# Identities of the two inverse buffers written by GpSimd, the first level ahead of the mirrored buffer, and VectorE copies over two PSUM banks

## The chip, the cores and the metric

The kernel runs on one core of a Trainium2 chip. The metric is the device time of one execution in microseconds. TensorE (PE) multiplies matrices into PSUM, VectorE (DVE) and ScalarE (ACT) read PSUM and SBUF, GpSimd (POOL) works on SBUF, and SyncE (SP) issues the loads and stores. Each engine works through its own instructions in the order written, and waits on semaphores for the others.

## The reference

Two blocks follow each other. The first has two hybrid attention layers; the change doesn't touch it. The second is a trunk layer with two recurrent branches over 512 tokens (256 of a context, 256 of a grid), each in two directions `d`, then a merge and an MLP.

```python
# branch A (rwkv7): 16 heads of 64
S_t = S_{t-1} diag(w_t) - (S_{t-1} kk_t) b_t^T + v_t k_t^T ;  y_t = S_t r_t
# branch B (gated delta rule), 8 heads of 128, in chunks of 64:
a_mat = tril(kb @ k^T * decay, -1) + I
sol = triangular_solve(a_mat, rhs)            # lower, unit diagonal
```

Both recurrences are evaluated chunk by chunk, and each chunk needs the inverse of a unit triangular matrix. These inverses are what the change is about.

## The kernel before

The program has stages L (first block), P (projections into `z_kept`), B (the recurrences) and C/M (merge and MLP). Stage B lasts from about 1890 to 2820 us of the span.

Stage B runs eight threads woven round robin by `Weave` on each engine: `thread_a(0)`, `thread_b(0)`, `thread_a(1)`, `thread_b(1)`, two tails and two bases. `thread_a(d)` goes over eight pairs of heads `c`, `thread_b(d)` over eight heads `h`; a thread of `d == 1` starts an inverse once the thread of `d == 0` is some steps into its own. Each engine's generator of a thread yields at the same places, so the weave alone fixes the order of the work on each engine, and the semaphores only hold it up. One round (two inverses of each branch) takes about 111.7 us and comes eight times.

An inverse of branch A (`inverse_a`, 8 blocks of 128, so 128x512 buffers) works on X (the inverse) and XP (its transpose, the *mirrored* buffer), both of which lie over buffers that the scores read before (Kd, Bd):

- VectorE copies an identity from `cst` into X and XP (L2734), after the last score matmuls (`sR`) and transposes (`tBt`).
- It writes level 0 into XP from NA (SBUF) by four predicated copies (L2742), then level 0 into X from PSUM by one (L2747), once TensorE has done the products `iq` of level 0, which move NA's diagonal blocks.
- For the levels 1 to 5, TensorE forms `iq` = NA X, VectorE takes the masked part into Q (L2759, one predicated copy for each of the thread's two banks), TensorE forms `it` (both products XP Q and Q XP), and ScalarE and VectorE share the copies back into X and XP (L1836, L1837, L2764, L2765). GpSimd restores Q to an identity (L3358) and at the end copies a part of XP into XT (L3362).

The inverse of branch B (`inverse`, 128x256) has the same steps: identities L2687, mirrored level 0 in L2694, level 0 of X in L2703. There X and XP lie over `g.gl`, which VectorE reads for NA (L2953); GpSimd writes `g.gl` and masks `g.dec` beforehand (L3404, L3407). The scores of branch A are masked out of PSUM in `scores` (L2855: two copies of 128x512 for NA and two for AK; L2863: four of 128x256 for RB and RK). The base tile's mixing of the next pair's tokens stands in L2601 and L2608.

In this document *iq0* and *iq1* are the `iq` products of levels 0 and 1, *Q1* is VectorE's masked copy of level 1, and *it1* the products that need it. The queue order on TensorE around the start of an A inverse is: score matmuls `sR`, iq0, matmuls of other threads, iq1, matmuls of other threads, it1.

```python
for x in (X, XP):                                            # L2733
    e.tensor_copy(x.rearrange("p (u s) -> p u s", u=8), bc(C("id64"), 8)).then_inc(*mark(V))
```

Of the kernel before, what the change touches and what calls it, by code (L numbers as in the profile page):

```python
# [6 lines left out]
F32 = mybir.dt.float32  # L7
# [241 lines left out]
def program(nc, W, WSM, LORA, PARd, CSTd, MSKd, CTX, XIN, XS, ZS, OUT):  # L249
    ctx = ExitStack()  # L250
    with ctx:  # L251
# [12 lines left out]
        banks = [ctx.enter_context(nc.psum_tensor(f"bank{i}", [128, 512], F32))[:, :] for i in range(8)]  # L264
# [289 lines left out]
        STRAIGHT = (slice(0, 4, 3), slice(0, 4, 2))  # L554
        CROSSED = (slice(1, 3), slice(1, 4, 2))

        def staying(lv):
            return slice(0, 2) if lv < 5 else slice(0, 4, 2)

        def moving(lv):  # L560
            return slice(2, 4) if lv < 5 else slice(1, 4, 2)

        def units(pairs):
            return [2 * s + i for s in range(4)[pairs] for i in range(2)]
# [3 lines left out]
        def tensor(e):  # L568
# [428 lines left out]
            def inverse(tag, ring, NA, X, XP, Q, n):  # L997
# [52 lines left out]
            def inverse_a(tag, ring, NA, X, XP, Q):  # L1050
# [23 lines left out]
                yield  # L1074
                for lv in range(1, 6):
                    straight, crossed = units(STRAIGHT[lv % 2]), units(CROSSED[lv % 2])
                    stay, move = units(staying(lv)), units(moving(lv))
                    w.wait_ge(done("X", tag, lv - 1))
                    w.wait_ge(done("Xc", tag, lv - 1)) if lv > 1 else None
                    b0, b1 = bank(), bank()  # L1080
                    for i in range(4):
                        u, v = straight[i], crossed[i]
                        for h in range(2):
                            mm(b0[halves[h], cols(i)], block(u, h), X[halves[h], cols(u)], True, True)
                        for h in range(2):
                            t = mm(b1[halves[1 - h], cols(i)], block(v, h), X[halves[h], cols(v)], True, True)
# [5 lines left out]
                    b0, b1 = bank(), bank()  # L1092
                    q = Q[lv % 2]
                    for i in range(4):
                        u, v = straight[i], crossed[i]
                        for h in halves:
                            mm(b0[h, cols(i)], XP[h, cols(u)], q[h, cols(u)], True, True)
                        for h in range(2):
                            mm(b1[halves[1 - h], cols(i)], XP[halves[h], cols(v)], q[halves[h], cols(v)], True, True)
                    for i in range(4):  # L1100
                        u, v = stay[i], move[i]
                        for h in halves:
                            mm(b0[h, cols(4 + i)], q[h, cols(u)], XP[h, cols(u)], True, True)
                        for h in range(2):
                            t = mm(b1[halves[1 - h], cols(4 + i)], q[halves[h], cols(v)], XP[halves[h], cols(v)], True, True)
# [305 lines left out]
        def scalar(e):  # L1411
# [412 lines left out]
            def inverse_a(tag, ring, X, XP, XT):  # L1824
# [5 lines left out]
                for lv in range(1, 6):  # L1830
                    ring.take(), ring.take()
                    yield
                    (b, u), _ = ring.take(), ring.take()
                    wd = 1 << lv
                    w.wait_ge(done("it", tag, lv))
                    cp(pairs(X, 4, wd, d)[:, STRAIGHT[lv % 2]], pairs(b[:, 0:256], 2, wd, d)).then_inc(*mark(V, "X", tag, lv))  # L1836
                    cp(pairs(XP, 4, wd, 1 - d)[:, staying(lv)], pairs(b[:, 256:512], 2, wd, 1 - d)).then_inc(*mark(V, "free", ring.name, u))  # L1837
                    counts.at[("XT", tag, lv)] = counts.last(V)
# [307 lines left out]
        def vector(e):  # L2146
# [531 lines left out]
            def inverse(tag, ring, NA, X, XP, XT, Q, n, sem, before):  # L2678
# [5 lines left out]
                for point in before:  # L2684
                    w.wait_ge(point)
                for x in (X, XP):
                    e.tensor_copy(x.rearrange("p (u s) -> p u s", u=n), bc(C("id64"), n)).then_inc(*mark(sem))  # L2687
                own(sem)
                m0 = M("xt0", d * 32, 32)[:, None, :].broadcast_to([128, n, 32])
                for h in (0, 64):  # L2690
                    hs = slice(h, h + 64)
                    xv = XP[hs, :].rearrange("p (u n two) -> p u n two", u=n, two=2)[:, :, :, 1 - d]
                    nv = NA[hs, :].rearrange("p (u n two) -> p u n two", u=n, two=2)[:, :, h // 2:h // 2 + 32, 1 - d]
                    e.copy_predicated(xv, m0[hs], nv).then_inc(*mark(sem))  # L2694
                counts.at[("XT", tag, 0)] = counts.last(sem)
                for lv in range(6):
# [5 lines left out]
                    if lv == 0:  # L2702
                        e.copy_predicated(region(X, wd, d), mk, src).then_inc(*mark(sem, "free", ring.name, u))  # L2703
                        counts.at[("X", tag, 0)] = counts.last(sem)
                        yield
# [21 lines left out]
            def inverse_a(tag, ring, NA, X, XP, XT, Q, before):  # L2727
# [3 lines left out]
                for point in before:  # L2731
                    w.wait_ge(point)
                for x in (X, XP):  # L2733
                    e.tensor_copy(x.rearrange("p (u s) -> p u s", u=8), bc(C("id64"), 8)).then_inc(*mark(V))  # L2734
                own(V)
                for h in range(2):
                    hs = slice(64 * h, 64 * h + 64)
                    nv = NA[hs, :].rearrange("p (s u n two) -> p s u n two", s=4, u=2, two=2)[:, :, :, 32 * h:32 * h + 32, 1 - d]
                    m0 = M("xt0", d * 32, 32)[hs, None, None, :].broadcast_to([64, 2, 2, 32])
# [1105 lines left out]
```

## Time and profile before

| | |
|---|---|
| median of 3 runs | 3774.3 us (3773.59 to 3777.36) |
| the profiled execution | 3773.41 us, of which its span 3771.5 us |
| mean granted TensorE clock | 0.975 |
| PE, PEld busy | 95%, 83% of the span |
| DVE, ACT, POOL busy | 59%, 40%, 44% |

A row of the timeline is: start, duration, engine, line, operation, out<-in, how many in the row, and in brackets how long the engine sat idle before it and on whom it waited. A row of several instructions has the time from the first one's start to the last one's end; neighbouring instructions of one engine can overlap, since the next begins before the last has drained. All numbers are microseconds unless said otherwise.

### The profile page before, as it was taken

What the parts mean: (1) busy time and instruction counts of PE and PEld (TensorE: products, weight loads), DVE (VectorE), ACT (ScalarE), POOL (GpSimd) and SP (SyncE); (2) the same over time, 40 slices, a digit from 0 to 9 for tenths busy, and PEclk for the clock granted to TensorE, in tenths of its full rate; (3) what the DMA queues carried; (4) which work ended last, traced back from release to release, by engine and by line L of the source; (5) the groups of instructions that cost most, each with busy time, mean ns of one, the idle gap of its engine ahead of it and who ended that gap; (6) DMA issues with size and microseconds to landing.
All of it is one profiled execution on the core that took longest, in us unless ns stands there. A gap on an engine that the chain in (4) does not pass through costs nothing. (4 is left out here: it accounts for less than half of the span.)

```text
span 3771.5 us, 79181 instructions
## 1 busy us (share of the span) xinstructions
PE 3575.4 (95%) x33504; PEld 3118.9 (83%) x33504; DVE 2224.6 (59%) x4232; ACT 1521.8 (40%) x2753; POOL 1651.4 (44%) x1195
## 2 busy tenths in 40 slices
PE   7999998999997999999979999999979999999998
PEld 6888787888786888888868878888869898989897
DVE  4645535655536776677666677666656654445443
ACT  4444434444435432232223333333334453535353
POOL 5555455555554543333321111111116566666664
PEclk9999999999999999999989999999999999999999
DMA  6445554444344777778610000000006445455543
GB/s 229 183 168 189 186 196 156 178 179 181 146 176 168 257 268 257 252 257 292 215 40 18 24 28 29 25 24 15 3 33 254 174 179 190 179 190 180 188 180 134
DMA packets 116368, 586.83 MB, mean 156 GB/s; under 512 B 20912, under 2 KB 40368, under 8 KB 51376
## 3 DMA queue, kind: packets, MB, share of 16 engines
q1 hardware_dynamic: 116016, 581.76, 42.2%
q8 instruction: 267, 4.37, 0.5%
q14 instruction: 85, 0.70, 0.1%
HBM read 561.00 MB, written 20.71 MB: 154 GB/s over the span
## 5 line engine op out<-in xcount | busy, mean ns | idle before, releaser
L574 PE MATMUL bank<-act_L,part_L 128*128 128x512 f32 (+1 forms) x4864 | 935.4, 347 | 9.2 <-DMA cst<-in_cst 4.8
L574 PEld LDWEIGHTS bank<-act_L,part_L 128*128 128x128 f32 x4864 | 756.1, 191 | 146.4 <-issue 28.1
L574 PE MATMUL bank<-act_P,part_P 128*128 128x512 f32 (+1 forms) x3488 | 716.4, 365 | 17.5 <-POOL part_P L3221 12.6
L3221 POOL TENSOR_TENSOR part_C<-wring,part_C 128x512 fp32r<-128x512 f32 x320 | 567.8, 1783 | 362.3 <-ACT part_C L1420 362.3
L3221 POOL TENSOR_TENSOR part_L<-wring,part_L 128x512 fp32r<-128x512 f32 x304 | 526.2, 1732 | 446.1 <-ACT part_L L1420 438.2
L574 PEld LDWEIGHTS bank<-act_P,part_P 128*128 128x128 f32 x3488 | 590.3, 188 | 136.9 <-DVE arena_P L2590 16.1
L574 PE MATMUL bank<-arena_B 64*64 64x64 f32 (+2 forms) x11200 | 446.0, 237 | 51.1 <-DVE arena_B L2747 24.8
L3221 POOL TENSOR_TENSOR part_P<-wring,part_P 128x512 fp32r<-128x512 f32 x184 | 306.3, 1670 | 427.7 <-ACT part_P L1420 427.7
L1420 ACT ACTIVATE part_C<-wring 128x1024 fp32r<-128x1024 f32 x320 | 338.0, 1057 | 347.9 <-PE bank L574 345.7
L574 PE MATMUL bank<-act_Y,part_C 128*128 128x258 f32 (+1 forms) x3840 | 464.8, 283 | 9.4 <-POOL part_C L3221 9.4
L574 PEld LDWEIGHTS bank<-act_Y,part_C 128*128 128x128 f32 x3840 | 463.9, 191 | 9.8 <-issue 9.6
L574 PEld LDWEIGHTS bank<-arena_B 64*64 64x64 f32 (+2 forms) x11200 | 380.7, 147 | 103.5 <-DVE arena_B L2747 27.2
L574 PE MATMUL bank<-act_C,part_C 128*128 128x512 f32 (+1 forms) x2560 | 459.6, 340 | 0.0
L574 PEld LDWEIGHTS bank<-act_C,part_C 128*128 128x128 f32 x2560 | 391.6, 188 | 58.0
L1420 ACT ACTIVATE part_L<-wring 128x1024 fp32r<-128x1024 f32 x304 | 320.7, 1056 | 255.6 <-PE bank L574 255.0
L2167 DVE TENSOR_TENSOR part_L<-wring,part_L 128x512 fp32r<-128x512 f32 x304 | 248.2, 816 | 254.7 <-ACT part_L L1420 253.5
L2167 DVE TENSOR_TENSOR part_C<-wring,part_C 128x512 fp32r<-128x512 f32 x320 | 235.0, 734 | 252.2 <-ACT part_C L1420 245.4
L2167 DVE TENSOR_TENSOR part_P<-wring,part_P 128x512 fp32r<-128x512 f32 x184 | 170.1, 925 | 189.9 <-ACT part_P L1420 189.8
L2228 DVE SCALAR_TENSOR_TENSOR arena_P<-arena_P,mods 128x512 f32<-128x512 f32 x240 | 272.7, 1136 | 8.9 <-DMA arena_P<-in_w 5.5
L1420 ACT ACTIVATE part_P<-wring 128x1024 fp32r<-128x1024 f32 x184 | 190.9, 1051 | 153.1 <-PE bank L574 152.4
L574 PE MATMUL bank<-wring,arena_B 64*64 64x64 f32 (+3 forms) x2208 | 193.1, 254 | 7.5 <-DVE arena_B L2855 3.1
L3358 POOL COPY arena_B<-cst 128x256 f32<-128x256 f32 x80 | 33.3, 416 | 379.1 <-PE bank L574 379.1
(262 smaller groups left out, 3595.1 us busy)
## 6 DMA issues: line engine op xcount, KB each, us to landing
wring<-in_w SPq DMA_DIRECT2D x404, 1024.0 KB, 4.9
arena_P<-in_w SPq DMA_DIRECT2D x64, 1024.0 KB, 5.2
mring<-in_w SPq DMA_DIRECT2D x32, 1024.0 KB, 6.6
z_kept<-arena_P SPq DMA_DIRECT2D x34, 256.0 KB, 5.7
z_kept<-arena_P SPq DMA_DIRECT2D x58, 128.0 KB, 5.6
xT<-z_kept SPq DMA_DIRECT2D x26, 256.0 KB, 2.7
arena_C<-z_kept SPq DMA_DIRECT2D x32, 128.0 KB, 2.8
cst<-z_kept SPq DMA_DIRECT2D x24, 128.0 KB, 2.1
```

The lines of the kernel that those rows point to most:

```text
L574: return e.matmul(out, lhsT, rhs, start=start, stop=stop)
L1420: return e.activation(out, a, ACT.Copy, scale=scale)
L2167: tt(wl[:, 0:4, :], wring[s % NS][:, 8 * j:8 * j + 4, :], wh[:, 0:4, :].bitcast(F32), sub).then_inc(*mark("dve_lo", "lov", stage, h))
L2228: z = ts(a, x, c, None, mult, None) if row == 0 else stt(a, x, c, a, mult, add)
L3221: e.tensor_tensor(wl[:, 4:8, :], wring[s % NS][:, 8 * j + 4:8 * j + 8, :], wh[:, 4:8, :].bitcast(F32), sub).then_inc(*mark("pool_lo", "lop ...
L3358: e.tensor_copy(region(Q[lv % 2], wd, d), same).then_inc(*mark(sem, "qf", tag, lv))
```

## The change

- GpSimd's `inverse` now writes the two identities. It waits for the events `sR` and `tBt` (branch A) or `NA` (branch B) and marks `xid` after X and `xpid` after XP, at the point of the weave where its stream of this inverse begins. VectorE waits for these marks.
- VectorE writes level 0 of X first (it needs `xid` and iq0), then the mirrored level 0 of XP.
- TensorE's iq1 of branch B no longer waits for XP's level 0.
- The eight banks are one PSUM tensor, so that one instruction can span a thread's two banks: one copy of 128x1024 in place of two of 128x512 for each of NA and AK, two of 128x512 in place of four of 128x256 for RB and RK, one of 128x256 in place of two of 128x128 for Q at each level. Q, X and XP are laid out by bank for that; TensorE does the same number of matmuls. Both banks are now marked free by the one copy.

```diff
-        banks = [ctx.enter_context(nc.psum_tensor(f"bank{i}", [128, 512], F32))[:, :] for i in range(8)]
+        psum = ctx.enter_context(nc.psum_tensor("bank", [128, 4096], F32))[:, :]
+        banks = [psum[:, 512 * i:512 * i + 512] for i in range(8)]
...
+        def two_banks(d):
+            return psum[:, 1024 * d:1024 * d + 1024].rearrange("p (b c) -> p b c", b=2)
...
             def inverse(tag, ring, NA, X, XP, Q, n):      # TensorE
-                    w.wait_ge(done("XT", tag, lv - 1)) if one else None
+                    w.wait_ge(done("XT", tag, lv - 1)) if one and lv > 1 else None
...
             def inverse_a(...):                           # VectorE
-                for point in before:
-                    w.wait_ge(point)
-                for x in (X, XP):
-                    e.tensor_copy(x.rearrange("p (u s) -> p u s", u=8), bc(C("id64"), 8)).then_inc(*mark(V))
-                own(V)
-                for h in range(2):
...
-                        e.copy_predicated(xv, m0, nv[:, which]).then_inc(*mark(V))
+                w.wait_ge(done("xid", tag))
                 b, u = ring.take()
                 w.wait_ge(done("iq", tag, 0))
...
                 counts.at[("X", tag, 0)] = counts.last(V)
+                w.wait_ge(done("xpid", tag))
+                for h in range(2):
...
+                    e.copy_predicated(home[:, 0:4:3], m0, nv[:, 0:4:2]).then_inc(*mark(V))
+                    e.copy_predicated(gone[:, 1:3], m0, nv[:, 3:0:-2]).then_inc(*mark(V))
+                counts.at[("XT", tag, 0)] = counts.last(V)
...
-                    for (b, u), which in zip(use, (STRAIGHT, CROSSED)):
-                        e.copy_predicated(q[:, which[lv % 2]], mk, pairs(b[:, 0:256], 2, wd, d)).then_inc(*mark(V, "free", ring.name, u))
+                    e.copy_predicated(by_side(Q[lv % 2], 0, wd, d), mk, in_banks(two_banks(d), wd, d)).then_inc(*mark(V, "Q", tag, lv))
...
             def scores(c, d):                             # VectorE
-                    for k, (b, u) in enumerate(use):
-                        e.copy_predicated(dst[:, 512 * k:512 * k + 512].rearrange("p (u t) -> p u t", u=4), bc(sm, 4),
-                                          b.rearrange("p (u t) -> p u t", u=4)).then_inc(*mark(V, "free", ring.name, u))
+                    e.copy_predicated(dst.rearrange("p (u t) -> p u t", u=8), bc(sm, 8),
+                                      psum[:, 1024 * d:1024 * d + 1024].rearrange("p (u t) -> p u t", u=8)).then_inc(
...
-            def inverse(tag, XP, XT, Q, n, sem):          # GpSimd
+            def inverse(tag, X, XP, XT, Q, n, sem, *before):
                 d = tag[-1]
+                for event in before:
+                    w.wait_ge(done(*event))
+                for nm, dst in (("xid", X), ("xpid", XP)):
+                    e.tensor_copy(dst.rearrange("p (u s) -> p u s", u=n), bc(C("id64"), n)).then_inc(*mark(sem, nm, tag))
                 yield
```

How the order of VectorE's instructions moves where an A inverse of `d == 0` begins (arena_B and wring are SBUF, bank is PSUM). Before:

```order
L2855 COPY_PREDICATED arena_B<-msk,bank 128x512 [waits s_pe_score]
L2855 COPY_PREDICATED arena_B<-msk,bank 128x512
L2975 SCALAR_TENSOR_TENSOR arena_B<-bank,par,arena_B 128x128 [waits s_pe_chain]
L2863 COPY_PREDICATED arena_B<-msk,bank 128x256 [waits s_pe_score]
L2863 COPY_PREDICATED arena_B<-msk,bank 128x256 x3
L2869 MEMSET wring 128x128
L2734 COPY arena_B<-cst 128x512 x2
L2742 COPY_PREDICATED arena_B<-msk,arena_B 64x2x64 [waits s_dve_rwkv]
L2742 COPY_PREDICATED arena_B<-msk,arena_B 64x2x64 x3
L2747 COPY_PREDICATED arena_B<-msk,bank 128x256 [waits s_pe_inv]
L2983 SCALAR_TENSOR_TENSOR arena_B<-arena_B,par,bank 128x128 [waits s_dve_gdn,s_pe_chain]
L2759 COPY_PREDICATED arena_B<-msk,bank 128x2x32x2 [waits s_pe_inv]
```

And now, with level 0 of X (L2746) ahead of the mirrored copies (L2755, L2756):

```order
L2865 COPY_PREDICATED arena_B<-msk,bank 128x1024 [waits s_pe_score]
L2987 SCALAR_TENSOR_TENSOR arena_B<-bank,par,arena_B 128x128 [waits s_pe_chain]
L2874 COPY_PREDICATED arena_B<-msk,bank 128x512 [waits s_pe_score]
L2874 COPY_PREDICATED arena_B<-msk,bank 128x512
L2881 MEMSET wring 128x128
L2746 COPY_PREDICATED arena_B<-msk,bank 128x256 [waits s_pe_inv,s_pool_rwkv]
L2755 COPY_PREDICATED arena_B<-msk,arena_B 64x2x64 [waits s_pool_rwkv]
L2756 COPY_PREDICATED arena_B<-msk,arena_B 64x128
L2755 COPY_PREDICATED arena_B<-msk,arena_B 64x2x64
L2756 COPY_PREDICATED arena_B<-msk,arena_B 64x128
L2995 SCALAR_TENSOR_TENSOR arena_B<-arena_B,par,bank 128x128 [waits s_dve_gdn,s_pe_chain]
L2765 COPY_PREDICATED arena_B<-msk,bank 128x128x2 [waits s_pe_inv]
```

The two copies from `cst` are gone, L2746 stands where they stood, and the order behind the mirrored copies is as it was. Next, GpSimd's queue where an A inverse of `d == 1` begins. Before:

```order
L3404 TENSOR_TENSOR arena_B<-arena_B,cst 128x512 [waits s_act_gdn]
L3407 TENSOR_TENSOR arena_B<-arena_B,cst 128x256 [waits s_pool_gdn]
L3358 COPY wring<-cst 128x4x32 [waits s_pe_inv]
L3362 COPY arena_B<-arena_B 64x4x64 [waits s_dve_gdn]
L3226 TENSOR_TENSOR smalls<-smalls,nhalf 128x8 [waits s_dve_rwkv]
L3358 COPY arena_B<-cst 128x128x2 [waits s_pe_inv]
```

And now:

```order
L3421 TENSOR_TENSOR arena_B<-arena_B,cst 128x512 [waits s_act_gdn]
L3424 TENSOR_TENSOR arena_B<-arena_B,cst 128x256 [waits s_pool_gdn]
L3374 COPY wring<-cst 128x4x32 [waits s_pe_inv]
L3366 COPY arena_B<-cst 128x512 [waits s_pe_score]
L3366 COPY arena_B<-cst 128x512
L3378 COPY arena_B<-arena_B 64x4x64 [waits s_dve_gdn]
L3238 TENSOR_TENSOR smalls<-smalls,nhalf 128x8 [waits s_dve_rwkv]
L3374 COPY arena_B<-cst 128x128x2 [waits s_pe_inv]
```

Here the identities (L3366) stand behind both mask products of branch B and the last restoring of Q of another inverse, and ahead of the copy into XT (L3378). At `d == 0` they stand behind that copy into XT alone, with the Q of level 1 next.

## Rows read from the trace of the kernel before

**Rows 1.** Busy time by stretch: PE, PEld, DVE, ACT, POOL, then clock, DMA.

```profile
2361.70:2473.40 111.70, 102.44 (x2098) 90.53 (x2096) 78.39 (x212) 42.13 (x126) 19.43 (x33) 0.95 0.08 25
2370.50:2396.90 26.40, 25.94 (x667) 22.29 (x667) 15.01 (x50) 10.41 (x34) 4.06 (x8) 1.00 0.01 3
...
2421.50:2438.00 16.50, 14.74 (x319) 13.32 (x320) 10.70 (x31) 5.28 (x17) 2.26 (x3) 0.90 0.23 67
```

**Rows 2.** Who waited for whom on PE in one round (2348.64 to 2460.30).

```profile
PE bank L574 <- DVE arena_B L2747: 3.4, 2, 1.9
```

**Rows 3.** Timeline of PE where the A inverse of `d == 0` begins.

```profile
2364.43 1.58 PE L574 MATMUL bank<-wring,arena_B 64*128 64x128 f32 x18 [0.44 <-DVE arena_B L2855]
...
2366.61 1.15 PE L574 MATMUL bank<-cst,arena_B 64*64 64x64 f32 x32
...
2370.49 0.69 PE L574 MATMUL bank<-arena_B 64*64 64x64 f32 x32 [1.86 <-DVE arena_B L2747]
```

**Rows 4.** Timeline of DVE at the same place.

```profile
2362.96 1.33 DVE L2855 COPY_PREDICATED arena_B<-msk,bank 128x512 f32<-128x512 uint8 x2 [0.67 <-PE bank L574]
...
2365.63 1.43 DVE L2863 COPY_PREDICATED arena_B<-msk,bank 128x256 f32<-128x256 uint8 x4 [1.11 <-PE bank L574]
...
2367.11 0.69 DVE L2734 COPY arena_B<-cst 128x512 f32<-128x512 f32 x2
2367.84 1.84 DVE L2742 COPY_PREDICATED arena_B<-msk,arena_B 64x128 f32<-64x128 uint8 x4
...
2370.24 0.31 DVE L2983 SCALAR_TENSOR_TENSOR arena_B<-arena_B,par,bank 128x128 f32<-128x128 f32 x1
2371.25 0.73 DVE L2759 COPY_PREDICATED arena_B<-msk,bank 128x128 f32<-128x128 uint8 x2 [0.70 <-PE bank L574]
```

**Rows 5.** Timeline of DVE where the A inverse of `d == 1` begins.

```profile
2307.37 1.65 DVE L2601 SCALAR_TENSOR_TENSOR arena_B<-xT,par,arena_B 128x512 f32<-128x512 f32 x1
...
2309.14 1.08 DVE L2734 COPY arena_B<-cst 128x512 f32<-128x512 f32 x2
2310.26 1.92 DVE L2742 COPY_PREDICATED arena_B<-msk,arena_B 64x128 f32<-64x128 uint8 x4
2312.21 0.72 DVE L2747 COPY_PREDICATED arena_B<-msk,bank 128x256 f32<-128x256 uint8 x1
2312.74 1.08 DVE L2953 SCALAR_TENSOR_TENSOR arena_B<-arena_B,cst,bank 128x128 f32<-128x128 f32 x4
```

**Rows 6.** Timeline of POOL at the same place.

```profile
2307.38 1.09 POOL L3404 TENSOR_TENSOR arena_B<-arena_B,cst 128x512 f32<-128x512 f32 x1 [5.23 <-ACT arena_B L1417]
2308.55 0.96 POOL L3407 TENSOR_TENSOR arena_B<-arena_B,cst 128x256 f32<-128x256 f32 x1
2309.46 0.48 POOL L3358 COPY wring<-cst 128x128 f32<-128x128 f32 x1
2309.89 0.59 POOL L3362 COPY arena_B<-arena_B 64x256 f32<-64x256 f32 x1
```

**Rows 7.** POOL around the inverse of `d == 0` (next after it), and the Q copy alone.

```profile
2373.46 0.42 POOL L3358 COPY arena_B<-cst 128x256 f32<-128x256 f32 x1 [15.54 <-PE bank L574]
...
2413.08 0.29 POOL L3358 COPY wring<-cst 128x128 f32<-128x128 f32 x1 [4.66 <-PE bank L574]
```

**Rows 8.** Line L3466: GpSimd's identity copies of 128x512 (min/median/max, ns).

```profile
L3466 POOL COPY arena_B<-cst x2: 616/842/1068, 1897.8 to 1898.4; 128x512 f32<-128x512 f32 x2
```

**Rows 9.** Timeline of PE at iq1 of the B inverse of `d == 1`.

```profile
2321.92 0.68 PE L574 MATMUL bank<-arena_B 64*64 64x64 f32 x16 [0.19 <-DVE arena_B L2703]
```

**Rows 10.** Timeline of DVE, `d == 1`: from level 0 to a later copy, in two rounds.

```profile
2325.86 0.29 DVE L2764 COPY arena_B<-bank 128x128 f32<-128x128 f32 x1 [2.48 <-PE bank L574]
...
2421.48 1.93 DVE L2742 COPY_PREDICATED arena_B<-msk,arena_B 64x128 f32<-64x128 uint8 x4
...
2438.01 0.29 DVE L2764 COPY arena_B<-bank 128x128 f32<-128x128 f32 x1 [2.48 <-PE bank L574]
```

**Rows 11.** The page's part 5: GpSimd's 128x512 products of stage L.

```profile
L3221 POOL TENSOR_TENSOR part_L<-wring,part_L 128x512 fp32r<-128x512 f32 x304 | 526.2, 1732 | 446.1 <-ACT part_L L1420 438.2
```

More of the change, by code:

```diff
@@ L551, in program, with by_side, in_banks @@
         CTXAT = (6, 8, 10, 12)
[L554 to L564, printed above, removed]
+        STRAIGHT = ((0, 1), (0, 2))
+        CROSSED = ((2, 3), (1, 3))
+        PLACE = (0, 2, 3, 1)
+        def two_banks(d):
+            return psum[:, 1024 * d:1024 * d + 1024].rearrange("p (b c) -> p b c", b=2)
+        def by_side(buf, lv, wd, side):
+            order = "p (b i m two w) -> p b i m two w" if lv % 2 == 0 else "p (i b m two w) -> p b i m two w"
+            return buf.rearrange(order, b=2, i=2, two=2, w=wd)[:, :, :, :, side, :]
+        def in_banks(bb, wd, side):
+            return bb[:, :, 0:256].rearrange("p b (i m two w) -> p b i m two w", i=2, two=2, w=wd)[:, :, :, :, side, :]
         GLA_LEAD, GLA_MORE = 3, 2
@@ L2676, in early, with inverse @@
                 yield from base_a_tile(0)
-            def inverse(tag, ring, NA, X, XP, XT, Q, n, sem, before):
+            def inverse(tag, ring, NA, X, XP, XT, Q, n, sem):
                 d = tag[-1]
@@ L2704, in inverse @@
                         counts.at[("X", tag, 0)] = counts.last(sem)
+                        mirror()
                         yield
@@ L2725, in inverse, with inverse_a @@
                 yield
-            def inverse_a(tag, ring, NA, X, XP, XT, Q, before):
+            def inverse_a(tag, ring, NA, X, XP, XT, Q):
                 d = tag[-1]
@@ L2730, in inverse_a @@
                 me, e_ = slice(64 * d, 64 * d + 64), 64 - 64 * d
[L2731 to L2743 removed]
+                w.wait_ge(done("xid", tag))
                 b, u = ring.take()
@@ L3379, in thread_a @@
                         counts.at[("qf", (c, d), lv)] = counts.at[("qf", (c - 1, d), old) if c else ("qid", d)]
-                    yield from weave.after(8, ("middle", c) if d == 0 else None, inverse((c, d), g.XP, g.XT, g.Q, 8, "pool_rwkv"))
+                    yield from weave.after(8, ("middle", c) if d == 0 else None, inverse(
+                        (c, d), g.X, g.XP, g.XT, g.Q, 8, "pool_rwkv", ("sR", c, d), ("tBt", c, d)))
                     for _ in range(12):
@@ L3414, in thread_b @@
                         counts.at[("qf", ("g", h, d), lv)] = counts.at[("qf", ("g", h - 1, d), old) if h else ("gqid", d)]
-                    yield from weave.after(8, ("middleb", h) if d == 0 else None, inverse(("g", h, d), g.XP, g.XT, g.Q, 4, "pool_gdn"))
+                    yield from weave.after(8, ("middleb", h) if d == 0 else None, inverse(
+                        ("g", h, d), g.X, g.XP, g.XT, g.Q, 4, "pool_gdn", ("NA", ("g", h, d))))
                     for _ in range(12):
```

108 lines of the change are left out of this document (61 added, 47 removed).

## The prediction

> **What bounds the kernel now.** The change lies in stage B alone, so I read that stage: busy time by stretch, then who waited for whom, then the timelines around the starts of the inverses, engine by engine. The rounds repeat: in one of 111.7 us TensorE is busy for 102.4, VectorE for 78.4 and GpSimd for 19.4 [rows 1]. So neither engine is the bound alone: TensorE waits a little in a few places, and only what shortens one of those waits, or the work that makes it, shortens the round. The largest is the wait for L2747, level 0 of X: 3.4 us in two waits of a round, the longer 1.9 [rows 2]. One wait is where the A inverse of `d == 0` begins (TensorE idle for 1.86 ahead of iq1 [rows 3]), the other, some 1.5, where that of `d == 1` begins. These are the places at which the change takes work off VectorE.
>
> A gain at `d == 0` is carried on whole. From iq1 on TensorE is busy for 25.94 of 26.40 us [rows 1], so everything behind it there is released by that run; and stage C starts its loads and products only after B, so that B's gain is the kernel's. I count eight rounds alike. The first begins with GpSimd a little busier, and I make no difference for it.
>
> **The A inverse of `d == 0`.** Before, VectorE goes from the identities (2367.11) over the mirrored copies (2367.84) to level 0 of X, whose end frees iq1 at 2370.49; Q1 starts at 2371.25, 0.07 after iq1's end at 2371.18 [rows 3, 4]. Three things change.
> - The identities leave VectorE. GpSimd has nothing to do here: before its next instruction, at 2373.46, it had been idle for 15.54 [rows 7]. It can begin when the score matmuls are done, which is when VectorE's L2863 starts (2365.63 [rows 4]). The form 128x512 from `cst` took 0.616 at its fastest, 1.068 at its slowest [rows 8]; I take 0.61, since the slow one is from a stretch in which VectorE was writing too, and the Q copies agree (0.42 for 256 columns [rows 7]). X is ready at 2366.3, XP at 2366.9: ahead of their readers, so these two copies cost nothing. If they took 1.07 each, XP would be ready at 2367.8, still in time.
> - Level 0 of X can't take the place of the identities at once, because it also waits for iq0, the matmuls of 2366.61 that end at 2367.76 [rows 3]. The merged score copies bring that forward: four copies of 256 columns took 1.43, two of 512 took 1.33 for as many columns [rows 4], so an instruction fewer saves some 0.05, and NA and AK together 0.10 (TensorE waits for AK's copy here: 0.44 [rows 3]; bounds 0 and 0.2). X starts at 2367.76 - 0.10 + 0.07 = 2367.73. The mirrored copies begin 0.53 behind it (as L2953 begins behind L2747 [rows 5]), at 2368.26, and end after 1.87 at 2370.13; L2983 takes 0.31 [rows 4], so VectorE reaches Q1 at 2370.44.
> - Iq1 moves ahead of this. TensorE is free at 2370.49 - 1.86 = 2368.63 [rows 3], X is done by 2368.45, and iq1's 0.69 ends near 2369.3. It is no longer what Q1 waits for.
>
> Q1 starts 0.81 earlier and, as one instruction, is 0.05 shorter. TensorE then waits for it ahead of it1: the stall has moved from iq1 to it1 and shrunk. Gain: **0.86 a round**, not the 1.86 that stood ahead of iq1.
>
> **The A inverse of `d == 1`.** Here VectorE isn't waiting for matmuls, and TensorE's queue goes from iq1 to the products that need L2953. What counts is when L2953 starts, 2312.74 before [rows 5]. GpSimd's queue has two mask products and a Q copy ahead of the identities: they end at 2309.51 and 2309.94 [rows 6]. The last took 0.48 there, but 0.29 alone [rows 7], and VectorE's copies that ran beside it are gone: 2309.75. X is ready at 2310.36 and XP at 2310.97. VectorE is there at 2309.14 [rows 5] and stands idle for 1.3. Level 0 of X starts at 2310.43, the mirrored copies at 2311.04 (0.07 for each semaphore); they take 1.95 (2310.26 to 2312.21 [rows 5]), and L2953 starts at 2312.99, **0.25 later than before**. The merged score copies, upstream of GpSimd's queue too, give back 0.10. Loss: **0.15 a round**. The earlier iq1 gives TensorE nothing, since its next wait is for L2953.
>
> **The rest.** In the B inverses VectorE loses two copies of 256 columns, but TensorE's run around them has one wait, 0.19 at `d == 1` [rows 9]; level 0 of X now stands ahead of the mirrored copies, and the wait goes: 0.19. GpSimd has their identities ready in time: NA is written by 2313.8 [rows 5], some six us before they are needed. The merged copies of Q save 0.05 each, ten in a round, but TensorE works at something else during nearly all; where VectorE runs dense, in the convolutions, one counts: 0.05 (bounds 0 and 0.5). RB and RK end 0.1 earlier, ahead of a wait. That the order moved as described is seen in the rows of the change, so that it doesn't do what it says is no case.
>
> **The sum.** 0.86 + 0.19 + 0.05 - 0.15 = 0.95 a round, 7.6 us in eight. Against the profiled execution, 3773.4 - 7.6 = 3765.8; the median of the runs is 0.9 higher, hence **3766.7**. A measurement of this kernel can tell a difference of 0.2%, 7.5 us: below 3766.8 is faster, above 3781.8 slower. The forecast lies on the lower border.
>
> One more term is even on both sides. In some rounds the granted clock falls to 1.2 GHz behind the stall at `d == 1`: from the mirrored copies to a later copy it took 15.60 at full clock (2310.26 to 2325.86 [rows 5, 10]) and 16.53 (2421.48 to 2438.01 [rows 10]) at a mean of 0.90 [rows 1]. Such a drop costs 0.93. The stall remains, and which rounds have it can change; four more or fewer are 3.7 us either way.
>
> **Rivals.**
> - *The whole stall goes.* If the products behind iq1 matter more than it1 (they carry the other threads' chains, and come up to 1.86 earlier), the gain is 1.86 + 0.10 + 0.19 + 0.05 - 0.15 = 2.05 a round: 3757.9. For it: the other threads wait for them. Against: TensorE's queue is in order, and it1 stands in it soon after. Chance 0.20.
> - *The mirrored copies are held by GpSimd.* At `d == 1` the copy into XT (L3362) follows the identities. VectorE's L2601 of 512 columns took 1.65 beside L3404 and ended 0.55 after it [rows 5, 6], where two copies of as many columns took 1.33 [rows 4]: an instruction with both inputs in SBUF can stand still while GpSimd works. The mirrored copies read mask and NA from SBUF. Held until 2310.97 + 0.59 = 2311.56, they lose 0.52 more: 3770.9. Against it: before, they started inside L3362 and took 0.08 more than at the other place [rows 4 to 6]. Chance 0.12. The Trainium skill has this as a rule (SBUF — State Buffer, Who interferes with whom): the pair of ports that VectorE and GpSimd share is an exclusive lock, held for the whole instruction, and a VectorE instruction with two SBUF inputs contends for it. By that rule L2601's 1.65 is expected, and the 0.08 is not.
> - *Slow GpSimd copies.* At 1.07 each, the slowest [rows 8], `d == 1` loses 2 x 0.46 = 0.92 more, and a round gains 0.03: 3774.1. Chance 0.10.
> - *GpSimd becomes the bound (slower).* With a price p of a copy, `d == 1` loses 2(p - 0.61) more, and above p = 1.33 XP is late at `d == 0` as well. GpSimd's products of 512 columns took 1.73 in stage L [rows 11]; at that price `d == 1` loses 2.24 and `d == 0` 0.80: 2.09 a round, 3791.0. It decides from p = 1.44, over twice what the same form took at best. Chance 0.10.
>
> **How the numbers follow.** The forecast has the rest, 0.48, half of it below the border because of the clock and the bounds of the small terms. Faster: 0.20 + 0.24 = 0.44. Slower: 0.10. Same: 0.24 + 0.12 + 0.10 = 0.46. The range goes from the first rival, 3757, to just above the third, 3775, and leaves out the last one and the tails.
>
> **What would show it.** At `d == 0`: GpSimd's two copies end before 2367, VectorE waits some 0.6 for iq0, TensorE has no wait ahead of iq1 and one of some 1.2 ahead of it1. At `d == 1`: VectorE waits some 1.3 for GpSimd, and L2953 starts no earlier against the matmuls. The round is 110.7 instead of 111.7. The forecast is wrong if the round is under 110, or if the copies of 512 columns take over 0.8.

## The result and the profile after

The changed kernel takes **3795.05 us** (median of 4 runs, 3794.5 to 3795.45) against 3774.43 of the kernel before in the same session: ratio 1.0053, 95% interval 1.0036 to 1.0071. That is 20.6 us slower; the forecast was 7.6 us faster, and the time lies outside its range. The profiled execution took 3794.5 us, its span is 3792.7, the mean granted clock 0.964 (0.975 before).

Busy time by stretch, changed kernel (columns as in [rows 1]): a whole round, the 12 us behind the wait at `d == 1`, and two more stretches of the same round. Then, from the kernel before, the 12 us behind the wait that answers to it.

```profile
2260.30:2376.36 116.06, 108.53 (x2106) 96.15 (x2106) 75.33 (x187) 42.71 (x127) 22.75 (x41) 0.90 0.08 24
2318.20:2330.20 12.00, 11.96 (x168) 11.27 (x170) 6.05 (x16) 3.67 (x11) 2.92 (x4) 0.57 0.20 59
2290.00:2300.00 10.00, 9.09 (x97) 7.99 (x94) 9.38 (x22) 4.35 (x11) 3.57 (x4) 0.66 0.09 8
2348.00:2358.00 10.00, 9.36 (x170) 8.79 (x171) 6.65 (x20) 3.43 (x11) 2.50 (x4) 0.66 0.09 31
```

```profile
2312.20:2324.20 12.00, 10.64 (x232) 9.41 (x232) 8.72 (x27) 3.60 (x11) 2.05 (x2) 1.00 0.32 90
```

A round is 116.06 us instead of 111.7. VectorE is busy for 3.1 us less than in [rows 1], as planned; TensorE is busy for 6.1 us *more*, with as many matmuls. The clock column says why: 0.90 against 0.95. At 0.57 and 0.66 TensorE ran for most of a stretch at the lower level (1.2 GHz, 0.5 in this column).

Timeline of PE, changed kernel: the rows that answer to [rows 3], and the wait at `d == 1` with what follows it.

```profile
2318.24 0.81 PE L578 MATMUL bank<-wring,arena_B 128*128 128x128 f32 x4 [2.30 <-DVE arena_B L2965]
2318.85 1.06 PE L578 MATMUL bank<-cst 128*128 128x128 f32 x4
...
2372.44 1.58 PE L578 MATMUL bank<-wring,arena_B 64*128 64x128 f32 x18 [0.31 <-DVE arena_B L2865]
...
2375.05 1.15 PE L578 MATMUL bank<-cst,arena_B 64*64 64x64 f32 x32 [0.36 <-DVE arena_B L2874]
...
2379.18 1.79 PE L578 MATMUL bank<-arena_B 128*128 128x128 f32 x66 [0.51 <-DVE arena_B L2995]
```

The same place at `d == 1` in the kernel before:

```profile
2312.99 0.69 PE L574 MATMUL bank<-arena_B 64*64 64x64 f32 x32 [1.56 <-DVE arena_B L2747]
2313.88 0.71 PE L574 MATMUL bank<-wring,arena_B 128*128 128x128 f32 x4 [0.19 <-DVE arena_B L2953]
2314.43 0.61 PE L574 MATMUL bank<-cst 128*128 128x128 f32 x4
2315.22 0.66 PE L577 MATMUL bank<-cst,arena_B 128*128 128x128 f32 x4 [0.18 <-DVE arena_B L2608]
```

At `d == 0`, 0.44 and 1.86 have become 0.31, 0.36 and 0.51. At `d == 1` one wait of 2.30 has taken the place of three, 1.56 ahead of iq1 and 0.19 and 0.18 behind it. The four matmuls that read `cst` take 1.06 us at the low clock, where they took 0.61 at the full one.

Timeline of DVE, changed kernel, where the A inverse of `d == 1` begins (answers to [rows 5]).

```profile
2311.25 0.74 DVE L2612 SCALAR_TENSOR_TENSOR arena_B<-xT,par,arena_B 128x512 f32<-128x512 f32 x1
2312.15 0.29 DVE L2726 COPY arena_B<-bank 128x128 f32<-128x128 f32 x1 [0.16 <-PE bank L578]
2314.47 0.72 DVE L2746 COPY_PREDICATED arena_B<-msk,bank 128x256 f32<-128x256 uint8 x1 [2.03 <-POOL arena_B L3366]
2315.03 0.60 DVE L2755 COPY_PREDICATED arena_B<-msk,arena_B 64x128 f32<-64x128 uint8 x1
...
2317.07 1.12 DVE L2965 SCALAR_TENSOR_TENSOR arena_B<-arena_B,cst,bank 128x128 f32<-128x128 f32 x4
```

Timeline of POOL at the same place (answers to [rows 6]).

```profile
2311.34 1.59 POOL L3421 TENSOR_TENSOR arena_B<-arena_B,cst 128x512 f32<-128x512 f32 x1 [5.11 <-ACT arena_B L1424]
2313.01 0.64 POOL L3424 TENSOR_TENSOR arena_B<-arena_B,cst 128x256 f32<-128x256 f32 x1
2313.60 0.29 POOL L3374 COPY wring<-cst 128x128 f32<-128x128 f32 x1
2313.83 1.17 POOL L3366 COPY arena_B<-cst 128x512 f32<-128x512 f32 x2
2314.94 0.39 POOL L3378 COPY arena_B<-arena_B 64x256 f32<-64x256 f32 x1
```

Timeline of DVE, changed kernel, where the A inverse of `d == 0` begins (answers to [rows 4]), and then POOL there.

```profile
2371.09 1.30 DVE L2865 COPY_PREDICATED arena_B<-msk,bank 128x1024 f32<-128x1024 uint8 x1 [0.67 <-PE bank L578]
...
2373.65 1.34 DVE L2874 COPY_PREDICATED arena_B<-msk,bank 128x512 f32<-128x512 uint8 x2 [1.03 <-PE bank L578]
...
2376.32 0.73 DVE L2746 COPY_PREDICATED arena_B<-msk,bank 128x256 f32<-128x256 uint8 x1 [1.20 <-PE bank L578]
...
2379.04 0.72 DVE L2765 COPY_PREDICATED arena_B<-msk,bank 128x256 f32<-128x256 uint8 x1
```

```profile
2373.68 1.17 POOL L3366 COPY arena_B<-cst 128x512 f32<-128x512 f32 x2 [7.63 <-PE bank L578]
```

**The account.** I take the stretch from the first level 0 of X to the last. First the kernel before, then the changed one.

```profile
1925.00:2758.60 833.60, 762.78 (x15686) 672.82 (x15684) 583.57 (x1570) 314.17 (x938) 144.74 (x247) 0.95 0.07 21
```

```profile
1920.90:2778.20 857.30, 797.89 (x15677) 706.50 (x15678) 556.40 (x1376) 315.18 (x935) 169.38 (x306) 0.90 0.07 20
```

It grew by 23.7 us. TensorE's idle time (length less busy) fell from 70.8 to 59.4: the waits gave **11.4 us back**. Its busy time rose by **35.1 us**. Cut into windows of 4 us, each counted as twice (1 less its clock) of its length, the stretch has 76 us at 1.2 GHz before and 169 after. So 93 us more at the low clock go with 35 us more of busy time, 0.38 each. If all of TensorE's work took twice as long at the low clock, it would be 0.5 each; no run shows where the rest is saved.

Only half of the 93 us stand behind the wait at `d == 1`. In the 16 us from the start of level 0 of X there, added over seven rounds, the low time is 24 us before and 68 in the changed kernel; everywhere else in the stretch it is 52 and 101.

### The profile page after: what moved, and what is told of

The parts are those of the page before. It is cut to its first block and busy times, and to the rows that moved or that the text cites. A ratio compares the mean times of both kernels' runs of the same rounds, so it can differ in the third digit from the quotient of the medians.

```text
span 3792.7 us, 79028 instructions
## 1 busy us (share of the span) xinstructions
PE 3607.1 (95%) x33504; PEld 3151.3 (83%) x33504; DVE 2201.5 (58%) x4024; ACT 1523.5 (40%) x2753; POOL 1679.3 (44%) x1259
## 5 line engine op out<-in xcount | busy, mean ns | idle before, releaser
L578 PE MATMUL bank<-arena_B 64*64 64x64 f32 (+2 forms) x11200 | 460.8, 244 | 26.2 <-ACT wring L1427 7.4
L578 PEld LDWEIGHTS bank<-arena_B 64*64 64x64 f32 (+2 forms) x11200 | 396.9, 153 | 77.3 <-issue 16.5
L1427 ACT ACTIVATE arena_B<-bank 128x128 f32<-128x128 f32 (+4 forms) x376 | 118.0, 351 | 210.1 <-PE bank L578 141.7
```

Of the source, the lines that this page charges most:

```text
L578: return e.matmul(out, lhsT, rhs, start=start, stop=stop)
L1427: return e.activation(out, a, ACT.Copy, scale=scale)
```

## The experiments

The ratio in the table is that of the session's own runs of the kernel before (its medians lay between 3770.5 and 3775.9). Length, busy and idle are TensorE's in the stretch of the account; "low" is its time at 1.2 GHz, worked out as above. These four are from one execution, the profiled one. For two_alone that one took 3764.3 us, 8.8 above the median of its five (3754.7 to 3764.3), and for ids_two 3764.4, 8.7 below the median of its eleven (3764.4 to 3777.6): their rows don't describe the median. In all others it lies within 3.1 us of the median.

| kernel | median us | ratio (95%) | length | busy | idle | low |
|---|---|---|---|---|---|---|
| before | 3774.4 | | 833.6 | 762.8 | 70.8 | 76 |
| changed | 3795.05 | 1.0053 (1.0036 to 1.0071) | 857.3 | 797.9 | 59.4 | 169 |
| two_alone | 3755.5 | 0.9957 (0.9944 to 0.9969) | 824.9 | 758.9 | 66.0 | 69 |
| reorder_alone | 3773.2 | 0.9997 (0.9988 to 1.0006) | 836.8 | 779.1 | 57.7 | 129 |
| ids_alone | 3775.4 | 1.0003 (0.9994 to 1.0012) | 835.1 | 766.3 | 68.8 | 93 |
| ids_reorder | 3784.2 | 1.0023 (1.0014 to 1.0032) | 847.4 | 785.5 | 61.9 | 139 |
| reorder_two | 3759.6 | 0.9957 (0.9945 to 0.9970) | 823.0 | 764.4 | 58.6 | 91 |
| ids_two | 3773.1 | 0.9989 (0.9980 to 0.9998) | 825.9 | 760.6 | 65.3 | 79 |
| after_fill | 3757.4 | 0.9945 (0.9931 to 0.9959) | 820.9 | 773.4 | 47.5 | 67 |
| two_fill | 3759.9 | 0.9959 (0.9947 to 0.9972) | 824.9 | 776.4 | 48.5 | 66 |
| after_fill3 | 3752.5 | 0.9942 (0.9930 to 0.9955) | 816.8 | 759.7 | 57.1 | 60 |
| after_fill1 | 3793.1 | 1.0052 (1.0040 to 1.0065) | 857.9 | 801.8 | 56.1 | 170 |
| late | 3755.0 | 0.9948 (0.9934 to 0.9962) | 815.9 | 749.5 | 66.4 | 56 |
| late_more | 3774.6 | 1.0001 (0.9993 to 1.0010) | 833.4 | 757.2 | 76.2 | 74 |
| after_dense | 3770.5 | 0.9991 (0.9982 to 1.0000) | 831.4 | 768.9 | 62.5 | 84 |
| after_once | 3778.0 | 1.0007 (0.9998 to 1.0016) | 840.7 | 782.3 | 58.4 | 125 |
| before_dense | 3795.7 | 1.0065 (1.0051 to 1.0079) | 858.4 | 792.1 | 66.3 | 138 |
| early | 3734.0 | 0.9894 (0.9880 to 0.9907) | 798.8 | 743.8 | 55.0 | 43 |
| early_dense | 3746.3 | 0.9933 (0.9921 to 0.9946) | 806.5 | 750.5 | 56.0 | 43 |
| early_fill | 3748.4 | 0.9932 (0.9920 to 0.9944) | 810.7 | 762.3 | 48.4 | 52 |

### One part of the change, or two

The expectations name theories by letters. H: one long wait of TensorE at `d == 1`, here called the hole, lets the clock fall. G: what costs is VectorE's waiting for GpSimd's late identities. F: what costs is that both banks come free by one later copy. Later ones: C, the lost time is the clock's; W, it is in the waits and the clock only goes along.

The change has three parts: identities by GpSimd (ids), level 0 of X first (reorder), copies over two banks (two). Six kernels have one or two of them. The edits are pieces of the diff above; where a part is left out, its lines are as before:

```diff
 # without ids: VectorE, ahead of level 0 of X
+                for nm, dst in (("xid", X), ("xpid", XP)):
+                    e.tensor_copy(dst.rearrange("p (u s) -> p u s", u=8), bc(C("id64"), 8)).then_inc(*mark(V, nm, tag))
 # without reorder: the mirrored copies ahead of it again
-                        mirror()
+                mirror()
 # without two: banks apart
-                e.copy_predicated(by_side(Q[lv % 2], 0, wd, d), mk, in_banks(two_banks(d), wd, d))
+                    for (b, u), which in zip(use, (STRAIGHT, CROSSED)):
```

two_alone: 

> The copies over two banks alone (identities by VectorE, mirrored copies first). Theory H (the hole: TensorE stands still in one long piece at d == 1, and the granted clock falls behind it): no change in the hole, so the clock and the time stay, 3771 to 3777 us, round 111 to 112. Theory F (both banks come free by one later copy, and iq0 waits 0.36): slower by 0.4 x 8 = 3 us at least, 3777 to 3785. Theory G (GpSimd's late identities): 3771 to 3777.

reorder_alone: 

> Level 0 of X ahead of the mirrored copies alone (VectorE still writes the identities). Theory G (what costs is VectorE's 2.03 us of waiting for GpSimd at d == 1): faster, since iq1 of d == 0 starts up to 1.3 earlier and nobody waits for GpSimd: 3765 to 3772. Theory H: iq1 of d == 1 leaves the middle of TensorE's wait, which becomes one hole of some 1.8 us where 1.56 and 0.19 stood on either side of it; if it is the joined hole that lets the clock fall, the time is 3780 to 3795 and the low-clock time per round over 15 us.

ids_alone: 

> The identities by GpSimd alone (mirrored copies first, banks apart). Theory G: L2953 of d == 1 starts later by the wait for GpSimd, up to 1 us a round: 3778 to 3786, clock as before. Theory H: the wait ahead of iq1 grows from 1.56 to some 2.3, the clock falls behind it in every round: 3785 to 3800, low-clock time per round over 15 us.

ids_reorder: 

> The whole change without the copies over two banks. Theories G and H: as slow as the whole change, 3790 to 3800, with the hole of 2.3 us at d == 1. Theory F: what the copies over two banks lose comes back, 3780 or less.

reorder_two: 

> The whole change with VectorE writing the identities. By the time at the low clock: the hole at d == 1 is some 2.0 (as in the reordering alone), so the clock falls as there: 3765 to 3780. Theory G (GpSimd's late identities are what costs on top of it): 15 us or more below the whole change. If it is as slow as the whole change, the identities are innocent.

ids_two: 

> The whole change with the mirrored copies first. The wait ahead of iq1 at d == 1 is some 2.3, at d == 0 some 0.6. Theory C with the order to blame: 3755 to 3770. If the wait for GpSimd alone suffices for the low clock, 3780 or more.

No part is at fault by itself: alone they give -18.8, -1.1 and +1.2 us. Nor do they add up. The two-bank copies gain 18.8 alone and cost 10.9 on top of the other two (3784.2 to 3795.05); GpSimd's identities cost 1.2 alone and 35 on top of the others (3759.6 to 3795.05). Five of the six fell outside every band that was expected; reorder_two met one, G's. Theory F falls with two_alone, which it had 3 us slower or more and which was 18.8 faster; in ids_reorder the copies over two banks do give back 10.9, but 3784 is not the 3780 or less that it wanted. Theories H and G both wanted 3778 or more of ids_alone, which has the long wait (2.27 us) and the waiting for GpSimd and took 3775.4, and 3790 or more of ids_reorder. The idle column does what the waits say: the reordering takes 13 us off it. The time follows only with the low column beside it: reorder_alone has 13 us less idle time and 53 us more at 1.2 GHz, and the sum is nothing.

### Idle matmuls in the hole

```diff
                     bank(), bank()
+                    for _ in range(10 if lv == 1 and d == 1 else 0):        # 3, 1 in the others
+                        mm(upper[:, 256:384], cst[:, 0:128], cst[:, 128:256], True, True)
```

two_fill has five of them in both inverses, on the kernel of two_alone, ahead of the wait for X.

after_fill: 

> The whole change, with ten idle matmuls (128x128 from the constants into the unused half of a bank, some 0.2 us each) ahead of iq1 of d == 1, so that TensorE works through most of the hole of 2.30 us; what it computes otherwise is the same. Theory C (the lost time is the granted clock, and it falls because TensorE stands still there): the hole shrinks to some 0.3, the stretch at 1.2 GHz behind it (10.2 us a round) goes or shrinks to 3.4, and the time falls by 8 x 3 to 8 x 5 us although work was added: 3755 to 3772. Theory W (the lost time is in waits and queues, the clock only goes along): the time stays at 3795 or rises.

two_fill: 

> The copies over two banks alone, with five idle matmuls ahead of iq1 in both A inverses, inside the waits of 1.30 and 1.35 us. Theory C: less time at the low clock than the 116 us of stage B without them, and 3740 to 3754. Theory W: no change, 3755 to 3760.

after_fill3: 

> The whole change with three idle matmuls in place of ten ahead of iq1 of d == 1: the hole shrinks from 2.30 to some 1.7. Is it the size of the hole or its being there? In the kernel with the identities by VectorE a hole of 1.68 went with 3760 us. Theory C with the size deciding: 3757 to 3768. If any hole does it, or if it is GpSimd's work beside it that costs: 3785 or more.

after_fill1: 

> The whole change with one idle matmul (some 0.2 us) ahead of iq1 of d == 1: the hole shrinks from 2.30 to 2.1. Theory S (the rounds are in step: the drops depend on where the work of a round falls, and a small shift decides): it can leave 3795 by 10 us or more, to anywhere in 3750 to 3800. Theory H (the hole's size): 3793 to 3796, since 0.2 of 2.3 is little.

Eighty matmuls more that compute nothing made the kernel **37.7 us faster** (3795.05 to 3757.4). Twenty-four made it 42.5 faster, eight only 1.9. The low column fell from 169 to 67 and 60, and stayed at 170. That the lost time is the clock's is shown by this: the work only grew. In after_fill3 nearly all that came back is busy time (38.2 us less, idle 2.3 less); in after_fill it is 24.5 of busy and 11.9 of idle time. two_fill missed: 17.5 us of idle time gone against two_alone, 17.5 of busy time more, the low time 66 instead of 69, and no gain: the eighty matmuls put in cost as much as the waits that they filled.

### The hole made longer, without GpSimd

So far the hole's size could decide (theory H again; the idle matmuls had cut it to 1.82 us in after_fill1 and 1.36 in after_fill3). These two are reorder_two with two or four more identity copies on VectorE between level 0 of X and the mirrored copies of `d == 1`.

```diff
+                for _ in range(2 if d == 1 else 0):                         # 4 in late_more
+                    own(V)
+                    e.tensor_copy(XP.rearrange("p (u s) -> p u s", u=8), bc(C("id64"), 8)).then_inc(*mark(V, "xpid", tag))
```

late: 

> The whole change with VectorE writing the identities (3760 us), and two identity copies more into XP at d == 1, behind level 0 of X and ahead of the mirrored copies, which lengthens the hole from 1.68 to some 2.5 without any GpSimd. Theory C: the clock falls as in the changed kernel, 3785 to 3800, much more than the 0.8 x 8 = 6 us of added work. Theory W: 3764 to 3769.

late_more: 

> VectorE writes the identities, and four copies of XP more stand ahead of the mirrored ones at d == 1: a hole of some 4 us without GpSimd. By work alone 8 x 1.2 = 9 us above the kernel with two: 3764. Theory H with a higher threshold: the low clock of the changed kernel, 3790 or more. Theory S: no relation with the hole's size, 3755 to 3785.

Timeline of PE, kernel late, then kernel late_more: the wait at `d == 1`.

```profile
2305.98 1.22 PE L578 MATMUL bank<-wring,arena_B 128*128 128x128 f32 x4 [2.81 <-DVE arena_B L2974]
```

```profile
2310.43 1.22 PE L578 MATMUL bank<-wring,arena_B 128*128 128x128 f32 x4 [3.71 <-DVE arena_B L2974]
```

With a hole of 2.81 us the kernel is *faster* than with one of 1.68 (3755.0 against 3759.6), and its low time is 56 us. The theory that the hole's size alone decides, on which my expectation of late rested, falls. With 3.71 the low time is 74, less than half of the changed kernel's.

The traces say more if the low time is parted as in the account: behind the wait at `d == 1` (16 us from level 0 of X, seven rounds) and elsewhere.

| kernel | that wait | low behind it | low elsewhere |
|---|---|---|---|
| early | 0.96 | 0 | 43 |
| two_alone | 1.30 | 3 | 66 |
| after_fill3 | 1.36 | 0 | 60 |
| before | 1.56 | 24 | 52 |
| before_dense | 1.56 | 41 | 97 |
| reorder_two | 1.68 | 27 | 64 |
| after_fill1 | 1.82 | 68 | 102 |
| changed | 2.30 | 68 | 101 |
| after_dense | 2.30 | 41 | 43 |
| late | 2.81 | 27 | 29 |
| late_more | 3.71 | 65 | 9 |

The wait bears on it: where it was 1.36 or less, next to nothing stood behind it, and where it was longer each kernel had 24 us or more. But how much goes by no order of length, and in most of these kernels over half of the low time stands elsewhere, though the other waits of a round are shorter in the changed kernel (5.1 us in sum against 6.5).

### A nudge where TensorE does not wait

The remaining theory (S, in step): whether the clock falls at a wait depends on where in time the round's work lies, and the rounds can fall into step, so that each meets the drops at the same places. To test it I put three idle matmuls into each round ahead of iq3 of `d == 0`, where no wait stands; once with all waits of the changed kernel, once with those of the kernel before. after_once has the ten matmuls of after_fill in one round alone.

```diff
+                    for _ in range(3 if lv == 3 and d == 0 else 0):         # after_dense, before_dense, early_dense
+                    for _ in range(10 if lv == 1 and tag == (2, 1) else 0): # after_once
```

after_dense: 

> The whole change with three idle matmuls a round where TensorE is busy without a wait (ahead of iq3 of d == 0); the hole of 2.30 stays. By work alone 8 x 0.6 = 5 us slower: 3800 (theories H and W). Theory S: the round is shifted out of its step and the clock falls less in spite of the hole and of the added work, 3760 to 3790.

after_once: 

> The whole change with the ten idle matmuls ahead of iq1 of d == 1 in the third round alone. Theory H and W: that round is shorter by 4 us or not at all, the others keep 116.06: 3790 to 3795. Theory S: if the step is one that rounds fall back into, the others return to 116.06 and it is 3788 to 3795 as well; if it hangs by where the first rounds happened to end, the rounds behind it change for good: 3760 to 3785.

before_dense: 

> The kernel before with the same three idle matmuls. By the work alone 3774 + 5 = 3779. Theory S: the clock can differ either way, 3755 to 3795.

Timeline of PE, kernel after_dense: the hole is the changed kernel's to the hundredth, and yet the kernel is 24.6 us faster than the changed one, with more work (its low time is 41 us behind that wait and 43 elsewhere, against 68 and 101).

```profile
2313.50 0.71 PE L578 MATMUL bank<-wring,arena_B 128*128 128x128 f32 x4 [2.30 <-DVE arena_B L2967]
```

The kernel before, with the same nudge, loses more than the change did: 3795.7 us, 25 above its own runs in that session. Its waits have the sizes of [rows 2, 3]; PE's timeline of before_dense, then its busy time in three stretches, with the clock:

```profile
2317.93 0.69 PE L574 MATMUL bank<-arena_B 64*64 64x64 f32 x32 [1.56 <-DVE arena_B L2749]
...
2378.25 0.69 PE L574 MATMUL bank<-arena_B 64*64 64x64 f32 x32 [1.86 <-DVE arena_B L2749]
```

```profile
2320.00:2330.00 10.00, 9.79 (x172) 9.06 (x173) 4.72 (x15) 2.82 (x10) 2.05 (x2) 0.69 0.25 69
...
2350.00:2360.00 10.00, 10.00 (x155) 9.54 (x154) 5.67 (x19) 2.91 (x9) 2.30 (x4) 0.66 0.01 3
...
1922.30:2780.70 858.40, 792.07 (x15734) 700.98 (x15732) 584.05 (x1571) 314.55 (x938) 143.56 (x247) 0.92 0.08 20
```

The step itself is seen in the starts of level 0 of X. Timeline of DVE, changed kernel, then before_dense, three rounds each:

```profile
2144.20 0.73 DVE L2746 COPY_PREDICATED arena_B<-msk,bank 128x256 f32<-128x256 uint8 x1 [1.19 <-PE bank L578]
...
2260.26 0.73 DVE L2746 COPY_PREDICATED arena_B<-msk,bank 128x256 f32<-128x256 uint8 x1 [1.19 <-PE bank L578]
...
2492.36 0.73 DVE L2746 COPY_PREDICATED arena_B<-msk,bank 128x256 f32<-128x256 uint8 x1 [1.19 <-PE bank L578]
```

```profile
2261.40 0.72 DVE L2749 COPY_PREDICATED arena_B<-msk,bank 128x256 f32<-128x256 uint8 x1
...
2377.48 0.72 DVE L2749 COPY_PREDICATED arena_B<-msk,bank 128x256 f32<-128x256 uint8 x1
...
2493.54 0.72 DVE L2749 COPY_PREDICATED arena_B<-msk,bank 128x256 f32<-128x256 uint8 x1
```

Both kernels, of different work and waits, have rounds of 116.05 to 116.08 us (2260.26 less 2144.20; the next two 116.05 on average; 2377.48 less 2261.40; 2493.54 less 2377.48). The kernel before wanders between 110.6 and 112.4 instead, once its first rounds are over. In after_once the round with the one nudge and those behind it took 111.8, 111.6, 112.1, 112.0, and then 115.95: the step was left for four rounds, and fallen back into. That is the profiled execution. Its eleven stand in two groups, four from 3769.6 to 3773.5 and seven from 3778.0 to 3779.5, and only one of the second group has a trace. Both readings that its expectation set against each other hold in part.

### The wait at its root, and the fastest version

In the changed kernel the score matmuls that GpSimd's identities wait for are done at 2309.6, GpSimd is idle until 2311.34, and then works at two mask products first. So I moved the identities of `d == 1` one step of the weave earlier.

```diff
                     weave.said.add(("prep", c, d))
-                    for _ in range(4):
+                    for k in range(4):
+                        if d == 1 and k == 3:
+                            identities((c, d), g.X, g.XP, 8, "pool_rwkv", ("sR", c, d), ("tBt", c, d))
                         yield
```

early: 

> The whole change, with GpSimd's identities of the A inverse of d == 1 one step earlier in its queue, ahead of the two mask products of branch B. The score matmuls that they wait for are done 1.75 us before the first mask product starts (2309.59 against 2311.34 in the changed kernel), so they fit in GpSimd's idle time: VectorE doesn't wait 2.03 any more, and the hole of TensorE at d == 1 shrinks from 2.30 to 0.3 to 1.0. Theory C: the clock falls no more behind it, 3745 to 3757 us, as good as with the idle matmuls or a little better. Theory W: only the wait comes back, 8 x 1.3 to 2 us: 3779 to 3785.

early_fill: 

> The same, with idle matmuls also in the three waits of the base threads on ScalarE and GpSimd (0.46, 0.64 and 0.92 us: two, three and four matmuls of 128x128). Theory C: the remaining stretches at 1.2 GHz, 6.8 us each behind these waits, go as well: 5 to 15 us faster than without them. Theory W: the same or slower by up to 8.

early_dense: 

> The version with GpSimd's early identities, and three idle matmuls a round ahead of iq3 of d == 0, where TensorE doesn't wait. If its 3734 is its own (few holes, little low clock): 3736 to 3742, by the work alone 3739. If it is a lucky fall of its rounds: 3745 or more.

Timeline of POOL, then DVE, then PE, kernel early, `d == 1`:

```profile
2286.30 1.17 POOL L3365 COPY arena_B<-cst 128x512 f32<-128x512 f32 x2 [3.37 <-PE bank L578]
2288.02 1.61 POOL L3427 TENSOR_TENSOR arena_B<-arena_B,cst 128x512 f32<-128x512 f32 x1 [0.55 <-ACT arena_B L1424]
```

```profile
2289.83 0.73 DVE L2746 COPY_PREDICATED arena_B<-msk,bank 128x256 f32<-128x256 uint8 x1 [0.71 <-PE bank L578]
```

```profile
2293.50 0.71 PE L578 MATMUL bank<-wring,arena_B 128*128 128x128 f32 x4 [0.96 <-DVE arena_B L2965]
```

VectorE now waits for iq0, not for GpSimd; the hole is 0.96; the kernel takes **3734.0 us**, 1.1% less than before, and less than I expected. Against the changed kernel it has 4.4 us less idle time and 126 us less at the low clock, and again the clock is the larger part. How much of it is luck, early_dense tells only in part. Its median is 12.3 us above that of early (17 if each is taken against the kernel before of its own session, -41.2 and -24.2), and the nudge's own work is some 5. That is above my band for "its own" and inside the one for "a lucky fall". But the two executions with a trace lie only 8.1 us apart (3735.2 and 3743.3), nearly all of it busy time (6.7 more), and their low time is the same; what the slower ones of early_dense (up to 3748.6) lost is in no trace. At 3746.3 the kernel is still 24 us under the kernel before. So over half of the gain outlasts this nudge; part of the 3734 may not last through other edits. early_fill was badly aimed: of its nine idle matmuls a round only the three on ScalarE's 0.64 stood in a wait (the waits of 0.47 and 0.92 are still there; they belong to another thread). It tells only that idle matmuls outside waits cost their time.

## Why the prediction was wrong

**The step that failed** is the one called "even on both sides": "four more or fewer are 3.7 us either way". I had seen that a drop of the clock costs time and follows stalls, priced it by one pair of rounds at 0.93, and took its change as small and neutral. It was +93 us at 1.2 GHz, 35 us, over four times the gain forecast. What failed is the number of drops more than the price of one: the pair of rounds had 3.3 us at the low clock (16.50 us at a mean of 0.90) for its 0.93, that is 0.28 for each us, against 0.38 measured; but I allowed for four such drops more, some 13 us, and there were 93. And I looked for them behind the stall at `d == 1` alone, where 24 of the 76 us of the kernel before stand and 44 of the 93 were added. No rival held it either: none had the clock as its mechanism, and the one on the slower side (GpSimd the bound, price above 1.44) is refuted by the price, 0.59.

**The waits** came nearly as forecast. At `d == 0` the gain of 0.86 is 1.12 (0.44 and 1.86 to 0.31, 0.36 and 0.51). The stall moved from iq1 to it1, as said. What I missed is the 0.36: both banks come free with RB and RK's second copy, and iq0 waits for that. The wait ahead of it1 was 0.51, not 1.2, and VectorE waited 1.20 for iq0, not 0.6. The first rival, by which the whole stall goes, would have taken 1.96 off here; it did not happen.
At `d == 1` the loss was 0.37, not 0.15 (1.56, 0.19 and 0.18 to 2.30), and VectorE waited 2.03, not 1.3: the mask product L3421 (L3404 before) took 1.59 instead of 1.09, and VectorE arrived earlier, because now its own L2612 was the one not held (0.74 for 1.65). The B inverse's 0.19 came. In sum the idle time of a round fell by 1.04 (0.95 forecast; 8.40 to 7.36, added over the waits of the rounds that begin at 2258.0 before and 2260.3 after; the next round before has 8.84), in the whole stretch by 11.4 us.

**The prices** were near: two identity copies 1.17, so 0.59 each (0.61 taken), which also refutes the rival of slow copies; the merged copies 1.30 for 1.33 and 1.34 for 1.43. "The forecast is wrong if the round is under 110" looked to the wrong side: the round became 116.06 by another cause.

**The rival of the shared ports.** Its price was 0.52; the first mirrored copy took 0.60 beside GpSimd's L3378, the others 0.44: 0.16 lost. It stays small.

What is shown: the loss is time at the low clock (idle matmuls take it away), neither one part of the change alone nor the hole's size alone makes it, and a nudge with no wait to fill brings it to the kernel before and takes it from the changed one. What stays open is the rule by which the clock falls at one wait and not at another of the same size; nor do the runs show why the low time outside the wait at `d == 1` grew too. Why rounds settle on a few lengths was not tried either.

## What to carry to other kernels

Where TensorE is busy for nine tenths in a loop of short waits, split the time into idle time and busy time at each clock before judging an edit: a shorter wait shows in the first, and the second can move by more. Before such an edit is called good or bad, time it with a nudge too (a few idle matmuls where nothing waits); here that alone moved the kernel before by +25 us and the changed one by -25. And if a moved step ends in a new wait, look in the new owner's queue for idle time just ahead: one step earlier was worth 61 us here, most of it by the clock.

## What was not expected of the hardware

- Three idle matmuls a round, some 5 us of work in all, moved the time by 25 us, with either sign. Kernels of different work settled on the same round, 116.04 to 116.14 us (changed, before_dense, after_fill1), and others on another, 112.63 to 112.74 (late_more and reorder_alone for five rounds and more, after_dense for three).
- Which of two instructions was held, VectorE's with two SBUF inputs or GpSimd's mask product, changed with less than 0.1 us: VectorE took 0.74 and GpSimd 1.59 where VectorE began 0.09 earlier (2311.25, 2311.34; in early 0.74 and 1.61 with 0.08); VectorE 1.65 and GpSimd 1.09 where they began within 0.01 [rows 5, 6]. The Trainium skill has this (SBUF — State Buffer, Who interferes with whom): whoever issues first gets the shared pair of ports, and the order decides who blocks. The first two cases agree; in the third the starts (2307.37 for VectorE, 2307.38 for GpSimd) are too close to say who was first. I had read only that one.
